# Expert tiles gathered by quarter rows and turned by VectorE in 32x32 blocks instead of by TensorE, weights in 8 KB runs, ScalarE evictions, held loads

## The reference

```
h = modulate(rms_norm(x, norm_ffn_g[l]), sh2, sc2)        # y * (1 + scale) + shift, by feature
scores = sigmoid(h @ router_w); one group of 4 experts per token, the best 2 in it
gates  = the two scores, normalised
a = silu(h @ w_gate[e]) * (h @ w_up[e])                   # 1024 -> 256, 16 experts
y = (a * gate) @ w_down[e]                                # 256 -> 1024
x = x + g2 * y
```

## Time and profile before

| | |
|---|---|
| median of the three runs shown | 1674.31 us |
| profiled execution, its own time | 1671.73 us |
| its span, first to last instruction | 1669.9 us |
| mean granted TensorE clock | 0.974 of full speed |
| TensorE busy | 1544.7 us, 92% |
| VectorE busy | 821.9 us, 49% |
| ScalarE busy | 266.7 us, 16% |
| GpSimd busy | 246.1 us, 15% |
| DMA | 302.41 MB, 181 GB/s in the mean |

### The profile page before, as it was taken

One profiled execution on the slowest core, in us unless ns is written; L12 is line 12 of the kernel. 1 busy time (PEld: TensorE's weight loads), 2 busy tenths in 40 slices (PEclk: granted clock), 3 DMA queues, 4 the chain that ended last, 5 costly groups with the idle time before them and its releaser, 6 DMA issues.

```text
span 1669.9 us, 17355 instructions
## 1 busy us (share of the span) xinstructions
PE 1544.7 (92%) x5589; PEld 844.7 (51%) x5590; DVE 821.9 (49%) x1584; ACT 266.7 (16%) x526; POOL 246.1 (15%) x412
## 2 busy tenths in 40 slices
PE   5989999999998999999896999999899899999991
PEld 3764544447884444444443434345588444444440
DVE  2463587654326223223227798999543622322323
ACT  3200000000212111111130000012241211111112
POOL 2000000000001232322200000313000122332220
PEclk9999999999999999999998999999899999999996
DMA  9644057643118788898474454454111989778846
GB/s 334 202 146 159 26 160 249 208 128 124 51 76 301 253 262 228 237 320 245 75 240 114 112 143 120 114 146 111 55 51 76 345 268 342 184 208 262 251 88 226
DMA packets 201459, 302.41 MB, mean 181 GB/s; under 512 B 10517, under 2 KB 160113, under 8 KB 201408
## 3 DMA queue, kind: packets, MB, share of 16 engines
q1 hardware_dynamic: 179040, 222.71, 41.9%
q0 software_dynamic: 18800, 65.39, 15.8%
q10 hardware_dynamic: 3568, 13.63, 2.1%
HBM read 248.55 MB, written 53.10 MB: 181 GB/s over the span
## 4 chain that ended last, share of the span: by engine, by line
PE 74%; DVE 14%; DMA 6%; SPq 2%; issue 2%; ACT 1%; POOL 0%; POOLq 0%; DVEq 0%; ACTq 0%
PE bank L1139 19%; PE bank L990 19%; PE bank L1069 16%; PE bank L1154 10%; DVE R L1770 7%; DVE WX L1350 3%; PE bank L1121 2%; DMA xsum_scratch<-R,TSUM 2%; PE bank L1251 1%; SPq L462 1%; PE bank L1086 1%; DMA WX<-in_ada_w 1%; PE bank L973 1%; PE bank L1007 1%; SPq L463 1%
## 5 line engine op out<-in xcount | busy, mean ns | idle before, releaser
L990 PE MATMUL bank<-HTR,WX 128*128 128x512 f32 x1024 | 453.0, 599 | 6.0 <-DMA WX<-in_hyb_w_in 5.1
L1139 PE MATMUL bank<-WX,R 128*128 x784 | 346.5, 595 | 4.3 <-DMA WX<-in_moe_w_gate 2.3
L990 PEld LDWEIGHTS bank<-HTR,WX 128*128 128x128 f32 x1024 | 192.7, 191 | 245.5 <-issue 238.5
L1770 DVE SCALAR_TENSOR_TENSOR R<-R,PT 128x512 f32<-128x512 f32 (+18 forms) x288 | 231.2, 803 | 10.2
L1069 PE MATMUL bank<-WX,R 128*128 128x256 f32 x1024 | 230.5, 384 | 2.2 <-DVE R L1327 1.1
L1139 PEld LDWEIGHTS bank<-WX,R 128*128 128x128 f32 x784 | 145.7, 191 | 170.0 <-issue 170.0
L1327 DVE TENSOR_TENSOR R<-bank,R 128x256 f32<-128x256 f32 (+2 forms) x77 | 38.8, 504 | 366.9 <-ACT R L744 255.8
L1069 PEld LDWEIGHTS bank<-WX,R 128*128 128x128 f32 x1024 | 194.3, 192 | 31.6 <-issue 2.7
L1154 PE MATMUL bank<-WX,R 128*128 x408 | 183.8, 593 | 4.1 <-DVE R L1592 4.1
L1350 DVE SCALAR_TENSOR_TENSOR WX<-WX,CAB 128x256 f32<-128x256 f32 x280 | 135.8, 485 | 10.0
L1599 DVE SCALAR_TENSOR_TENSOR R<-bank,GSLOT,HTR 128x512 f32<-128x512 f32 x51 | 38.3, 751 | 166.5 <-DMA xsum_scratch<-R,TSUM 111.8
(11 more groups left out here) (212 smaller groups left out, 1082.5 us busy)
## 6 DMA issues: line engine op xcount, KB each, us to landing
WX<-in_ada_w SPq DMA_DIRECT2D x48, 1024.0 KB, 11.8
WX<-in_moe_w_gate SPq DMA_DIRECT2D x32, 1024.0 KB, 7.1
WX<-in_moe_w_up SPq DMA_DIRECT2D x32, 1024.0 KB, 12.3
WX<-in_moe_w_down SPq DMA_DIRECT2D x32, 1024.0 KB, 15.3
WX<-in_conf_w SPq DMA_DIRECT2D x20, 1024.0 KB, 9.3
WX<-glu_scratch SPq DMA_DIRECT2D x64, 260.0 KB, 4.5
WX<-in_hyb_w_in SPq DMA_DIRECT2D x10, 1024.0 KB, 12.0
xsum_scratch<-WX ACTq DMA_DIRECT2D x8, 1024.0 KB, 4.0
```

The lines of the kernel that those rows point to most:

```text
L990: ins = pe.matmul(dst[:], lhs(k), rhs(k), start=(k == 0), stop=(k == kc - 1))
L1139: ins = pe.matmul(M[0][:], XT[:, k, :], WX[:, bass.ds(at + k * 2 * FE, 2 * FE)], start=(k == 0), stop=(k == KC - 1))
L1770: link(dve.scalar_tensor_tensor(out=o[:, t0:HT], in0=p[:, HT * h + t0 - d:HT * h + HT - d], scalar=tap(CTAPS - 1 - d), in1=o[:, t0:HT], op ...
```

## The change

Each row of 1024 features is seen as four quarters of 256. For a tile, four indirect DMAs (c = 0 to 3) gather, for the 32 slots of group c, quarter a of the row to partition 32 a + t. VectorE then transposes 32x32 blocks with a stride of 8 in the source, so that feature 8 p + k of all 128 slots lies on partition p in block k (XTQ). ScalarE applies scale and shift for all 8 blocks into XT. The weights' gate and up rows are laid out by the same rule, feature 8 p + k on partition p, which makes one run of 8 rows, 8 KB. Scale and shift are brought into that layout through DRAM (MCT). The first tile of each layer is still gathered by whole rows (into XG0) and transposed by TensorE. The quarter row numbers (4 x row + quarter) are made by four small products with a selector and one VectorE operation.

Further: experts 1 and 2 are loaded when the first tile has been gathered; the last tile's output has a buffer of its own (YL) and its row numbers are copied ahead; gate_up waits for the second half of XT only before its fifth product; in step 2 of layer 1's first projection ScalarE evicts all eight pieces.

```diff
 # SyncE
-                g = i["moe_w_gate"][l].rearrange("e (k p) f -> e p k f", p=P)
-                u = i["moe_w_up"][l].rearrange("e (k p) f -> e p k f", p=P)
+                g = i["moe_w_gate"][l].rearrange("e (p k) f -> e p k f", p=P)
+                u = i["moe_w_up"][l].rearrange("e (p k) f -> e p k f", p=P)
...
-                sp.dma_start(wgu[:, :, 0:FE], pick(g)).then_inc(s, 16)
-                sp.dma_start(wgu[:, :, FE:2 * FE], pick(u)).then_inc(s, 16)
+                sp.dma_start(WXP[:, 3 * b, :, :], pick(g)).then_inc(s, 16)
+                sp.dma_start(WXP[:, 3 * b + 1, :, :], pick(u)).then_inc(s, 16)
...
-                    if e == NEB - 2:
-                        sp.wait_ge(xpj, 16 * (l + 1))
+                    if e == 1:
+                        sp.wait_ge(xg_in[l], 16)
 # GpSimd
+            pool.memset(QUARTER[:], 0.0).then_inc(const, 1)
+            for a in range(1, SH):
+                pool.wait_ge(const, 12 + a)
+                pool.affine_select(out=QUARTER[:], in_=QUARTER[:], ...).then_inc(const, 1)
...
+                def gather_quarters():
+                    for c in range(SH):
+                        pool.indirect_dma_start(
+                            out=XG[:, FE * c:FE * c + FE], out_offset=None, in_=xn4_dram,
+                            in_offset=bass.IndirectOffsetOnAxis(ap=TCUR4[:, c:c + 1], axis=0)
+                        ).then_inc(xq_in[l], 16)
...
                 def next_tile(t):
-                    pool.wait_ge(xg_in[l], t * 16 + 16)
-                    pool.tensor_copy(TCUR[:], TOKI[:, bass.ds(t + 1, 1)]).then_inc(cur_ok[l], 1)
-                    pool.wait_ge(cur_ok[l], t + 2)
-                    pool.wait_ge(xtr[l], t + 1)
+                    if not isinstance(t, int) or t > 1:
+                        pool.wait_ge(xq_in[l], t * (16 * SH) - 16 * SH)
+                        pool.wait_ge(xtr[l], t)
+                    pool.tensor_copy(TCUR4[:].unsqueeze(1), TOK4[:, bass.ds(t, 1), :]).then_inc(cur_ok[l], 1)
+                    pool.wait_ge(cur_ok[l], t + 1)
                     met()
-                    gather()
+                    gather_quarters()
...
+                def add_last(t):
+                    pool.wait_ge(xg_in[l], 16)
+                    pool.tensor_copy(TCUR[:], TOKI[:, bass.ds(t, 1)]).then_inc(sum_cur[l], 1)
+                    pool.wait_ge(sum_cur[l], t + 1)
+                    pool.wait_ge(ys_d[l], t + 2)
+                    pool.wait_ge(y_out[l], t * 16 + 16)
+                    met()
+                    send(TCUR, YL)
...
+                pool.wait_ge(lg, 4 * l + 4)
+                pool.tensor_copy(SEL, IDENT[:].rearrange("p (c i) -> p c i", c=SH).unsqueeze(2).broadcast_to(
+                    [P, SH, SH, CG])).then_inc(sel_ok, 1)
                 pool.wait_ge(tok_ok, l + 1)
                 pool.tensor_copy(TCUR[:], TOKI[:, 0:1]).then_inc(cur_ok[l], 1)
                 pool.wait_ge(cur_ok[l], 1)
-                gather()
+                gather_first()
+                pool.wait_ge(tok4_ok, l + 1)
+                next_tile(1)
                 pool.wait_ge(tab_ok, l + 1)
...
-                next_tile(0)
-                next_tile(1)
+                next_tile(2)
                 pool.wait_ge(x_out[l], 16 * 4)
                 with pool.Fori(0, more) as t:
-                    next_tile(t + 2)
+                    next_tile(t + 3)
                     add_rows(t)
                 add_rows(more)
-                add_rows(more + 1)
+                add_last(more + 1)
 # ScalarE
-            def evict_ht(r, l, ffn, h, beside=lambda k: None):
-                for k in range(0, KC, 2):
+            def evict_ht(r, l, ffn, h, beside=lambda k: None, ks=range(0, KC, 2)):
+                for k in ks:
...
-                def evict_tile(n_tr):
+                def turned_in(n_tr, of):
                     act.wait_ge(xtr[l], n_tr)
-                    for k in range(4):
-                        ins = act.activation(XT[:, k, :], TB_[0][:, k * P:(k + 1) * P], ACT.Identity,
-                                             bias=MC[:, l, 3, k:k + 1], scale=MC[:, l, 2, k:k + 1])
-                    ins.then_inc(xt_a[l], 1)
+                    for part, done in ((range(4), xt_a), (range(4, KC), xt_d)):
+                        for k in part:
+                            ins = act.activation(XT[:, k, :], of(k), ACT.Identity, bias=MCT[:, l, 1, k:k + 1],
+                                                 scale=MCT[:, l, 0, k:k + 1])
+                        ins.then_inc(done[l], 1)
...
                     act.activation(SG, M[0][:, 0:FE], ACT.Silu).then_inc(sg_ok[l], 1)
-                    evict_tile(t + 2)
+                    turned_in(t + 2, lambda k: XTQ[:, k * P:(k + 1) * P])
...
                 for p in range(4):
+                    if (l, p) == (0, 2):
+                        act.wait_ge(ada_fin, NADA)
+                        for n in range(NL):
+                            act.dma_start(mc_dram[n].rearrange("s (k p) -> p s k", p=P), MC[:, n, 2:4, :],
+                                          allow_slow_non_contiguous=True).then_inc(mc_out, 16)
+                    if (l, p) == (0, 3):
+                        act.wait_ge(mc_out, 16 * NL)
+                        act.dma_start(MCT[:]..., mc_dram.rearrange("l s (p k) -> p (l s) k", p=P)).then_inc(mc_in, 16)
...
                 if n == 2:
-                    evict_ht(2, 1, 0, 1)
+                    evict_ht(2, 1, 0, 1, ks=range(KC))
 # TensorE
+                pe.wait_ge(sel_ok, l + 1)
+                pe.wait_ge(idf_ok, l + 1)
+                for c in range(SH):
+                    ins = pe.matmul(X0[:, P + MAXT * c:P + MAXT * (c + 1)], SEL[:, c]..., IDF, start=True, stop=True)
+                ins.then_inc(sel_ps, 1)
...
                 def gate_up(t, e):
                     pe.wait_ge(xt_a[l], t + 1)
-                    pe.wait_ge(xt_d[l], t + 1)
...
                     for k in range(KC):
-                        ins = pe.matmul(M[0][:], XT[:, k, :], WX[:, bass.ds(at + k * 2 * FE, 2 * FE)],
+                        if k == 4:
+                            pe.wait_ge(xt_d[l], t + 1)
+                        ins = pe.matmul(hid, XT[:, k, :], WXP[:, bass.ds(at, 2), k, :],
                                         start=(k == 0), stop=(k == KC - 1))
...
-                transpose_tile(16)
+                transpose_first()
                 first_gate_up()
-                transpose_tile(32)
                 transpose_hidden(0)
...
                     gate_up(t, expert_of(t))
-                    transpose_tile(t * 16 + 32)
                     down(t - 1, buffer_at(expert_of(t - 1)))
                     transpose_hidden(t)
 # VectorE
+                dve.tensor_scalar(IDF, ids, SPARE[:], None, ALU.add).then_inc(idf_ok, 1)
...
+                dve.wait_ge(sel_ps, l + 1)
+                dve.tensor_scalar(TOK4..., X0[...], float(SH), QUARTER[:], ALU.mult, ALU.add).then_inc(tok4_ok, 1)
...
-                def evict_tile(n_tr):
...
+                def turn(t):
+                    dve.wait_ge(xq_in[l], t * (16 * SH))
+                    if not isinstance(t, int):
+                        dve.wait_ge(xt_d[l], t)
+                    dve.transpose(XTQ.rearrange("p (k c t) -> p k c t", k=KC, c=SH),
+                                  XG.rearrange("p (c q k) -> p k c q", c=SH, k=KC)).then_inc(xtr[l], 1)
...
                 hidden(0)
+                turn(1)
                 turned(0)
                 with dve.Fori(1, nt) as t:
+                    turn(t + 1)
                     hidden(t)
                     tile_out(t - 1)
                     turned(t)
-                tile_out(nt - 1)
+                dve.wait_ge(dn[l], nt)
+                rows_by(nt - 1, YL)
...
-                if n == 2:
-                    evict_ht(2, 1, 0, 1)
```

More of the change, by code:

```diff
@@ L303, in trunk @@
         rms_sd = sem("rms_root_ready")
+        mc_out = sem("moe_scale_shift_stored")
+        mc_in = sem("moe_scale_shift_by_row_group")
+        sel_ok = sem("quarter_selectors_made")
+        idf_ok = sem("row_numbers_ready")
+        sel_ps = sem("row_numbers_by_quarter")
+        tok4_ok = sem("quarter_row_numbers_ready")
+        xq_in = [sem(f"quarter_rows_in{l}") for l in range(NL)]
         xn_ok = sem("xn_ready")
```

76 lines of the change are left out of this document (47 added, 29 removed).

## The result

The changed kernel is slower: 1689.24 us in the median of ten runs (1680.7 to 1694.4) against 1672.35 us for the kernel before in the same series, a ratio of 1.0091 with a 95% interval of 1.0070 to 1.0112. I had said 1622, and faster. The profiled execution took 1690.15 us, its span is 1688.4 us, 18.5 more than before. I read its page first: part 4, the chain by engine and the head of the chain by line.

What follows compares the result with a forecast made beforehand. TensorE was taken to bound the kernel, with 74% of the chain and never idle in layer 0's expert loop. 1671.7 - 42.6 + 5 - 12.5 - 2.9 + 1.0 + 1.0 + 0.8 = 1621.5, said as 1622 us; range 1608 to 1660.

Steps and rivals of the forecast that it cites:

- GpSimd and the gathers, the real question: Expert loop: gather, landing and turn form a ring, 8.9 us alone, 11.4 beside a load, mean near 10.5 per tile.
- The turn: Expert loop: VectorE's block transpose of a gathered tile, 128x1024, taken as 1.3 us from bounds of 0.75 to 5.
- Rival 3: Expert loop: block transpose takes 4 us or more, mean period 12.2, about 1700 us; chance 0.05.
- the 5 us in which the turn may be late: Expert loop: the turn, nominally 2 us into gate and up, may end 5 us later, absorbing a single late tile.
- The loop's saving: Expert loop: eight transposes leave TensorE, 10.52 us per tile; 49 x 0.87 = 42.6 us less, 5 us given back.
- Rival 4: Expert loop: another wait holds TensorE some 0.9 us per tile; only idle stretch and tails gain, 1659 us; chance 0.05.
- Idle stretch: Layer 1's first projection: ScalarE's eight evictions start products 13.3 us earlier; 12.5 us gain taken, 6 at least.
- tails: End of each layer: with YL the last scatter goes out earlier, gain 1.4 us, twice: 2.9.
- What is added: Layer starts: routing 1.0 us, second tile turned later 1.0, GpSimd selectors 0.8; scale and shift through DRAM hidden.
- The held loads: Layer starts: expert 1 and 2 loads, begun after the first gather's issue, covered by 2 us at the least.
- Rival 1: Expert loop: rings bind in part, period 12 to 13 us beside a load, mean 10.8 to 11.4, 1632 to 1662; chance 0.25.
- rival 2: Expert loop: 1 KB gather rows wait behind 8 KB weight runs; mean period 13.1, 1744 us, 1680 at half severity; chance 0.08.

Runs made afterwards that it cites:

- e15: Changed kernel, normalised rows stored in DRAM in block order so the block transpose reads contiguous elements: 1662.71 us, ratio 0.9948 to the kernel before.
- e6: Changed kernel with a semaphore for each quarter, each turned when landed and its next gather issued once turned: 1634.92 us, ratio 0.9785 to the kernel before.
- e3: Changed kernel, loop's expert loads cut to 256 bytes per partition and matrix (wrong weights, only times count): 1625.15 us, ratio 0.9720 to the kernel before.
- e1: Kernel before with only ScalarE evicting all eight pieces in step 2 of layer 1's first projection: 1655.36 us, ratio 0.9909.
- e7: Changed kernel with two instead of four dummy products at the experts' start and the second tile turned before SiLU's product: 1675.51 us, ratio 1.0028 to the kernel before.
- e10: e9 with the loads of experts 1 and 2 not held until the first tile is gathered: 1635.89 us, ratio 0.9786 to the kernel before.
- e9: Changed kernel with the edits of e6 and e7 together, nothing left out: 1627.18 us, ratio 0.9731 to the kernel before.
- e14: e10 with gate and up weights read in 1 KB runs (features paired wrongly, only times count): 1623.60 us, ratio 0.9711 to the kernel before.
- e4: Changed kernel with gate and up weights loaded in 1 KB runs as before (mismatched features, only times count): 1680.76 us, ratio 1.0066 to the kernel before.
- e13: Changed kernel, contiguous transpose source with weights, scale and shift laid out for it, nine load issues per expert: 1723.27 us, ratio 1.0328 to the kernel before.

## Why the prediction was wrong

The step that failed is the one headed "GpSimd and the gathers, the real question", with its sentences "The ring is then 8.9 us alone and 11.4 beside a load" and "The mean is near 10.5". The mechanism was named rightly: a ring of its own that sets the pace beside loads. Its terms were too small. The turn took 2.03 us, not 1.3; turn to first issue and the issues 4.9, not 4.6; the landing beside a load 6.6 in the mean of the rings of 12.6 us and more (5.7 to 7.3), not 5.5. Alone the landing was 2.7 for my 3.0. That makes 9.6 and 13.5 instead of 8.9 and 11.4. Loads stand beside 27 of the 49 rings, fewer than the three tiles in four of my text, and still the mean ring is 11.7. Nor did my own terms give the 10.5 that I wrote: three tiles in four at 11.4 and one at 8.9 make 10.8. (Rival 3 has the opposite slip: its mean of 12.2 puts only one tile in four beside a load.) VectorE waited for quarters before 48 of its 51 turns, so it was the ring, and not TensorE, that set the mean. e15 prices the turn's term at 24 us, shown. e6 and e3 show that the rest hangs on the ring beside loads, since either cure brings most periods to 10.5.

A second part of the same step failed in kind. I took the 5 us in which the turn may be late as something that every late tile has anew. They are there once: against TensorE's 10.52 a ring beside a load loses 3.0 us and one alone wins back 0.9. Once they are used up VectorE stands waiting in the turn with SiLU's product behind it (the other order, the turn behind that product, was not tried), and a pause of TensorE is followed by products at a granted clock of 0.80. In gate and up of the loop, the second tiles among them, 17.8 us are longer products and 34.2 longer waits. My sum counted every late microsecond once.

**The loop's saving.** TensorE's own period is 10.52, as said, and the transposes' 0.87 us are gone. Neither ScalarE's eight evictions (3.2 us) nor the split wait cost anything on time. Rival 4 is out.

**The turn.** I chose 1.3 from bounds of 0.75 to 5, and measured 2.03. The page of the Trainium skill that I had set aside for the saving, VectorE: DVE Perf Modes, "The three transpose paths", gave an estimate of 2.5 us for bf16, nearer than mine; for a source without a stride mine was right (1.24).

**Idle stretch and tails.** The idle stretch was right: 13.6 for 12.5, shown by e1 alone (15.4). The tails' 2.9 for 2.9 is luck in its sum: 2.6 and 0.3 where I had 1.4 and 1.4.

**What is added.** Routing and GpSimd's start, 1.8 together, were 7.1; the second tile, 1.0 (with the two transposes saved, -0.7), was +5.3. e7 shows that 8.4 of these 12.4 come back at the starts by moving two things (1.7 + 2.0 + 2.2 + 2.5). I had counted instructions and not what stands behind them in order: dummy products that start after the selectors, and a turn that starts after SiLU. The scale and shift through DRAM left no trace in the order of the work. The held loads, which I had put down as covered, are a gain beside 8 KB runs: e10 without them is 8.7 us slower than e9. With 1 KB runs they are not needed (e14).

**Rivals.** Rival 1 was the right one, a period of 12 to 13 us beside loads; but I priced its mean at 11.4 at most and had it faster than before. The turning point of rival 2, a mean of 11.65 us, was passed (11.90 and 12.00) by rival 1's mechanism and not by the run size, as e4 shows. I gave 0.11 to slower.

## What to carry to other kernels

Before work is moved from the bound engine to a chain of other engines with one buffer, write that chain as a ring with the slowest of its terms beside the heaviest traffic, not the mean; here the ring was longer than the bound engine's period in half of the cases, and the mean of the kernel followed it. Cutting the ring (here, a semaphore and a reissue for each quarter) was worth more than shortening a term: 51 us against 24 by the ratios. A late tile cost its wait and then slower products (8.66 us for 6.87), and since VectorE works in order its wait was also paid by SiLU's product, which stood behind it. Where the chain of a profile does not add up to the whole span, ask where it was lost before comparing shares.

## What was not expected of the hardware

- VectorE's block transpose of 128x1024 float32: 2.03 us with a source stride of 8 elements, 1.24 without; in pieces of 128x256 0.61 and 0.42 each.
- Four gathers of 128 KB, issued 1.28 us apart, land 2.7 us after the last issue alone and 5.7 to 7.3 beside a load, the same for runs of 1 and of 8 KB. Stores of rows, though, landed after 12.9 us with nine loads in 8 KB runs issued ahead of them (e10), and after 9.2 with five in 1 KB runs (e14).
- SyncE issued nine loads of 1 MB in 8 KB and 4 KB runs within 7.3 us (e10, 508.48 to 515.74). With gate and up in 1 KB runs the fifth held it for 9.58 us and the sixth for 6.72 (e14).
- With gate and up read in rows of 1 KB, a packet of the weights' queue took 83 ns in the mean where each of these DMAs went to 32 partitions, in nine issues per expert (e13), and 64 ns where it went to 128, in three (e4). Which of the two makes the difference was not separated.
